# Rotation tables of a diagonal state-space layer, built by doubling on ScalarE and GpSimd in place of outer products on GpSimd alone

## What is computed

```python
mag = exp(lr * dt); abar = mag * (cos(li * dt) + 1j * sin(li * dt))
bu  = einsum('tgh,gph->tgp', u, bbar)        # drive of each state
x_t = abar * x_(t-1) + bu_t                  # scan over the 512 tokens
y   = Re(einsum('tgp,ghp->tgh', x, c)) + d * u
```

## Time and profile before

| | |
|---|---|
| runs, median (lowest to highest) | 3290.7 us (3290.01 to 3291.89) |
| the profiled execution | 3289.22 us, span 3287.4 us |
| PE, DVE, ACT, POOL busy in the profiled execution | 2939.9, 1758.0, 786.9, 531.4 us |
| the stage of interest | about 145 to 672 us of the span |

### The profile page before, as it was taken

How to read it: one execution, slowest core, us unless ns; L and a number is a source line. 1 busy time by engine, 2 the same in 40 slices (tenths; PEclk the granted TensorE clock), 3 DMA queues, 4 the chain that set the end, 5 groups by cost and what they waited for, 6 DMA issues and landing times. The chain is left out here.

```text
span 3287.4 us, 35120 instructions
## 1 busy us (share of the span) xinstructions
PE 2939.9 (89%) x13768; PEld 2205.4 (67%) x13768; DVE 1758.0 (53%) x2107; ACT 786.9 (24%) x1019; POOL 531.4 (16%) x411
## 2 busy tenths in 40 slices
PE   6999999987559958999999988899949999989897
PEld 4756666675228837888888765588828877765585
DVE  6799999965653365112553237522272157337433
ACT  4311111133432222111222213311122122213221
POOL 3365565515010041000000001000030000001000
PEclk8999999998679977999999999999959999999998
DMA  4667877761023141222433332222113254341321
GB/s 161 216 264 297 317 285 295 294 247 56 26 103 118 51 179 41 85 80 103 163 117 119 115 124 75 108 76 88 62 58 106 95 193 157 136 158 60 144 90 63
DMA packets 112852, 454.03 MB, mean 138 GB/s; under 512 B 11472, under 2 KB 20816, under 8 KB 76752
## 3 DMA queue, kind: packets, MB, share of 16 engines
q1 hardware_dynamic: 112720, 452.24, 37.5%
HBM read 380.36 MB, written 71.83 MB: 138 GB/s over the span
## 5 line engine op out<-in xcount | busy, mean ns | idle before, releaser
L2302 PE MATMUL ps<-h_hi,w_hi 128*128 128x512 f32 (+1 forms) x1792 | 661.6, 369 | 78.8 <-POOL h_lo L490 72.8
L2303 PE MATMUL ps<-h_lo,w_hi 128*128 128x512 f32 (+1 forms) x1792 | 645.0, 360 | 0.0
L2304 PE MATMUL ps<-h_hi,w_lo 128*128 128x512 f32 (+1 forms) x1792 | 640.8, 358 | 0.0
L2302 PEld LDWEIGHTS ps<-h_hi,w_hi 128*128 128x128 f32 x1792 | 344.9, 192 | 151.9 <-POOL h_lo L490 51.7
L384 PE MATMUL ps<-h_hi,w_hi 128*128 128x512 f32 (+1 forms) x1152 | 413.0, 358 | 37.7 <-DVE w_lo L337 37.7
L385 PE MATMUL ps<-h_lo,w_hi 128*128 128x512 f32 (+1 forms) x1152 | 412.2, 358 | 0.0
L2186 DVE TENSOR_TENSOR w_lo<-raw,w_hi 128x2048 fp32r<-128x2048 f32 x72 | 164.8, 2289 | 460.6 <-ACT w_hi L2137 460.6
L386 PE MATMUL ps<-h_hi,w_lo 128*128 128x512 f32 (+1 forms) x1152 | 410.0, 356 | 0.0
L2303 PEld LDWEIGHTS ps<-h_lo,w_hi 128*128 128x128 f32 x1792 | 346.1, 193 | 51.9 <-issue 6.0
L2304 PEld LDWEIGHTS ps<-h_hi,w_lo 128*128 128x128 f32 x1792 | 344.9, 192 | 51.3
L1475 POOL TENSOR_TENSOR wide<-ident_sb,stat 128x128 f32<-128x128 f32 x96 | 38.5, 401 | 1454.2 <-DVE stat L1535 1454.2
(11 more groups left out here) (305 smaller groups left out, 4333.7 us busy)
## 6 DMA issues: line engine op xcount, KB each, us to landing
raw<-w_in SPq DMA_DIRECT2D x112, 1024.0 KB, 5.1
raw<-ada_w SPq DMA_DIRECT2D x96, 1024.0 KB, 9.1
raw<-w_out SPq DMA_DIRECT2D x48, 1024.0 KB, 5.0
proj<-xw SPq DMA_DIRECT2D x60, 384.0 KB, 2.5
xw<-proj SPq DMA_DIRECT2D x70, 256.0 KB, 3.2
xw<-proj SPq DMA_DIRECT2D x46, 384.0 KB, 3.2
xw<-resid SPq DMA_DIRECT2D x8, 1536.0 KB, 12.2
proj<-wide SPq DMA_DIRECT2D x32, 256.0 KB, 11.2
```

The costliest lines, as they stand in the source:

```text
L2302: pe.matmul(a_[q], wh, h_hi[:, k, a:b], start=k == 0, stop=False)
L2303: pe.matmul(a_[q], wh, h_lo[:, k, a:b], start=False, stop=False)
L2304: ins = pe.matmul(a_[q], wl, h_hi[:, k, a:b], start=False, stop=k == KC - 1)
```

## The change

POOL no longer forms outer products. E[0..31] is copied to the head of `ee`, and four steps double the table: E[m..2m) = E[0..m) * E[m], for m = 32, 64, 128, 256. The factor E[m] is one number for each partition (the coarse power 1, 2, 4 or 8 of `e_sb`), so the four real products of a step are ACT activations with a scale from SBUF, into four half-size buffers `gt`; POOL does only the subtraction and the addition. ACT's `table(n+1)` stands between `w_hi` of slot n and the copies and `out_(n-1)` of that slot. Two semaphores are new: `turn_in` (ACT to POOL, products done) and `turn_out` (POOL to ACT, a step's sums done). Before the loop ACT does `table(0)` ahead of the first `w_hi`.

```diff
-            gt = [take(T) for _ in range(3)]
+            gt = [take(T // 2) for _ in range(4)]
...
-                        pool.wait_ge(st.sem, st.now)
-                        pool.tensor_tensor(g_[0], f_re, c_re, ALU.mult).then_inc(st.step(), 1)
...
-                        pool.tensor_tensor(ee[n % 2][1], gt[2], gt[1], ALU.add).then_inc(st.tell(e_ready, n + 1), 1)
+                        er, ei = ee[n % 2]
+
+                        pool.wait_ge(x_ready.h, x_ready.at(n - 1))
+                        pool.tensor_copy(er[:, 0:S_FINE], e_sb[:, j, 0, 0:S_FINE]).then_inc(st.step(), 1)
+                        pool.tensor_copy(ei[:, 0:S_FINE], e_sb[:, j, 1, 0:S_FINE]).then_inc(st.step(), 1)
+                        pool.wait_ge(st.sem, st.now)
+                        for s in range(4):
+                            m = S_FINE << s
+                            pool.wait_ge(turn_in.h, turn_in.at(4 * n + s + 1))
+                            pool.tensor_tensor(er[:, m:2 * m], gt[0][:, 0:m], gt[1][:, 0:m], ALU.subtract).then_inc(st.step(), 1)
+                            pool.wait_ge(st.sem, st.now)
+                            pool.tensor_tensor(ei[:, m:2 * m], gt[2][:, 0:m], gt[3][:, 0:m], ALU.add).then_inc(
+                                st.tell(e_ready, n + 1) if s == 3 else st.tell(turn_out, 3 * n + s + 1), 1)
+                            pool.wait_ge(st.sem, st.now)
...
+                    def table(n):
+
+                        i, j = divmod(n, 4)
+                        if j == 0:
+                            act.wait_ge(loaded[1].h, loaded[1].at(16 * (i + 1)))
+                        for s in range(4):
+                            m = S_FINE << s
+                            a = S_FINE + (1 << s)
+                            w_re, w_im = e_sb[:, j, 0, a:a + 1], e_sb[:, j, 1, a:a + 1]
+                            er, ei = (e_sb[:, j, c, 0:S_FINE] if s == 0 else ee[n % 2][c][:, 0:m] for c in range(2))
+                            if s:
+                                act.wait_ge(turn_out.h, turn_out.at(3 * n + s))
+                            else:
+                                act.wait_ge(e_ready.h, e_ready.at(n))
+                            act.activation(gt[0][:, 0:m], er, ACT.Copy, scale=w_re)
+                            act.activation(gt[1][:, 0:m], ei, ACT.Copy, scale=w_im)
+                            act.activation(gt[2][:, 0:m], er, ACT.Copy, scale=w_im)
+                            act.activation(gt[3][:, 0:m], ei, ACT.Copy, scale=w_re).then_inc(turn_in.h, 1)
+                    table(0)
                     for n in range(slots):
...
                         act.activation(w_hi[:, n % 2, :], raw[:, 0, :], ACT.Copy).then_inc(hi_done.h, 1)
+                        if n + 1 < slots:
+                            table(n + 1)
```

More of the change, by code:

```diff
@@ L206, in program @@
             "sq_added", "s_act", "s_vec", "ssm_in", "ssm_out", "cz_done", "e_done"))
+        turn_in, turn_out = count("turn_in"), count("turn_out")
         row_sums, sums_read, inverted = count("row_sums"), count("sums_read"), count("inverted")
@@ L965, in _ @@
                             pool.wait_ge(loaded[1].h, loaded[1].at(16 * (i + 1)))
[L966 to L970, removed]
@@ L971, in _ @@
-                        pool.wait_ge(st.sem, st.now)
-                        pool.tensor_tensor(g_[0], f_re, c_re, ALU.mult).then_inc(st.step(), 1)
-                        pool.tensor_tensor(g_[1], f_im, c_im, ALU.mult).then_inc(st.step(), 1)
-                        pool.wait_ge(st.sem, st.now)
-                        pool.tensor_tensor(g_[2], f_re, c_im, ALU.mult).then_inc(st.step(), 1)
-                        pool.wait_ge(x_ready.h, x_ready.at(n - 1))
-                        pool.tensor_tensor(ee[n % 2][0], gt[0], gt[1], ALU.subtract).then_inc(st.step(), 1)
@@ L979, in _ @@
-                        pool.wait_ge(st.sem, st.now)
-                        pool.tensor_tensor(g_[1], f_im, c_re, ALU.mult).then_inc(st.step(), 1)
-                        pool.wait_ge(st.sem, st.now)
-                        pool.tensor_tensor(ee[n % 2][1], gt[2], gt[1], ALU.add).then_inc(st.tell(e_ready, n + 1), 1)
+                        er, ei = ee[n % 2]
+                        pool.wait_ge(x_ready.h, x_ready.at(n - 1))
+                        pool.tensor_copy(er[:, 0:S_FINE], e_sb[:, j, 0, 0:S_FINE]).then_inc(st.step(), 1)
@@ L1140, in ssm_and_conditions @@
             for s, v in ((loaded[0], 32 * chunks), (loaded[1], 16 * chunks), (loaded[2], 16 * chunks), (b_ready, slots // 2),
-                         (b_read, slots), (e_ready, slots), (x_ready, slots), (y_out, chunks), (pair_used, slots // 2), (ada_used, per * slots), (ada_copied, 3 * LAYERS),
+                         (b_read, slots), (e_ready, slots), (turn_in, 4 * slots), (turn_out, 3 * slots), (x_ready, slots), (y_out, chunks), (pair_used, slots // 2), (ada_used, per * slots), (ada_copied, 3 * LAYERS),
                          (ada_turned, 3 * LAYERS), (mods_done, 3 * LAYERS), (hi_done, slots), (lo_done, slots),
```

## The result

Four runs of the changed kernel gave a median of 3390.9 us (3390.5 to 3395.4), four of the kernel before (the three above and one of 3284.6) 3290.4 us; the ratio is 1.031 (95% interval 1.029 to 1.033). Slower by 100.6 us, where 3391 us was forecast. The profiled execution took 3395.4 us, some 4 more than the median, so its stretches are a little long.

A forecast was written before the change was run, and what follows sets the result against it. DVE was taken as the bound, PE just behind. First chunk +18, six more +79, last +3 sum to +100, which on 3290.7 gives 3391 us; range 3325 to 3425.

The forecast's parts named there:

- the most that the change could bring: With DVE relieved, PE's 63.2 us a chunk against 65.2: 2.0 us for each of 8 chunks, about 16 us.
- walk of one chunk: Times through four slots from the end of the first drives: a chunk goes from 65.2 to 78.3 us, +13.1.
- POOL's last sums: End of each table, which `out_` was taken to follow; four later POOL operations meet DVE at 0.25 us each.
- The clock: PE's clock drops after long idleness at a boundary, costing its matmuls 1.0 + 0.5 = 1.5 us.
- the two ladders: Ordinary table: 11.4 us from the end of DVE's tile; first table of a chunk: 11.1 us from its powers landing.
- the low bound: Cheap end of every term, about +50 us, with powers landing 3 us earlier: worked out as 3320, given as 3325.
- two losses of its own: PE's main matmuls start late in each chunk: 5.0 us in slot 4i+1, 8.6 us at the boundary, slot 4i+3.
- the shut-out: A table's first POOL operations are kept from SBUF for all of DVE's `w_lo`, 2.3 us.
- Rival 2: Only boundaries cost, as `w_lo` does not shut POOL out: about +50, 3340 us; chance 0.25.
- Rival 1 (faster): `out_` is never late and PE becomes the bound: up to 16 us come back, 3275 us; chance 0.04.

The follow-up runs named there:

- experiment 1: The changed kernel with table(n+1) moved behind the copies and `out_(n-1)` on ACT; 3276.8 us, ratio 0.9962 to the kernel before.
- experiment 7: The changed kernel with six more unused ACT copies of 256 columns in each table; 3425.8 us, ratio 1.041 to the kernel before.
- experiment 8: The same six more ACT copies a table, in the changed kernel with table(n+1) moved behind `out_(n-1)`; 3279.9 us, ratio 0.9972.
- experiment 10: The changed kernel with three buffers for E and two tiles for the powers, `out_` still behind the table; 3285.1 us, ratio 0.9987.
- experiment 2: The kernel before without the outer products of 30 of its 32 tables, a one-column operation giving the signal; 3277.4 us, ratio 0.9966.
- experiment 4: The changed kernel with table(n+1) behind `out_(n-1)` and two tiles for the powers; 3277.5 us, ratio 0.9965.
- experiment 5: The changed kernel with table(n+1) behind `out_(n-1)` only in the last slot of each chunk (3, 7, ...); 3381.1 us, ratio 1.0281.
- experiment 6: The changed kernel with table(n+1) behind `out_(n-1)` only in the second slot of each chunk (1, 5, ...); 3371.2 us, ratio 1.0248.
- experiment 3: The changed kernel with two tiles for the powers, each load issued a chunk early; 3376.9 us, ratio 1.0271.
- experiment 9: The changed kernel with three buffers for E, so table(n+1) waits for DVE's tile n-2, `out_` still behind it; 3344.0 us, ratio 1.017.

## Why the prediction was right, and where not

The forecast and its mechanism held. PE waits for `out_`, `out_` stands behind the ladder on ACT (experiments 1, 7 and 8), and the ladder begins late for two reasons: table(n+1) waits for DVE's tile n-1, and at a boundary for the powers. Taking both away with the order left as it is (experiment 10) brings back 106 us where 101 had been lost, so all of it and a little of the gain. What the forecast called the most that the change could bring, about 16 us, measured about 12 (experiments 1, 2, 4). It was read from one chunk: from drives to drives the mean of six is 64.9 us in the kernel before, not 65.2, and 63.7 in experiment 1, where PE waits for nothing after slot 0, not 63.2.

Its walk of one chunk, against the chunk that begins at 313.64 in the trace after, the end of slot 8's drives:

| | forecast | trace |
|---|---|---|
| DVE's tile of slot 4i ends | 10.8 | 11.8 |
| main matmuls of 4i+1, late by | 23.6, 5.0 | 23.7, 5.1 |
| next drives done | 36.6 | 38.4 |
| powers land | 52.0 | 52.5 |
| main matmuls of 4i+3, late by | 63.8, 8.6 | 63.3, 6.3 |
| chunk (to the end of the next chunk's drives) | 78.3 | 78.6 |

The agreement is better than the working deserves: three of its terms were off and cancel, which is luck.
- **The end of the ladder that counts.** The working let `out_` wait for POOL's last sums. ACT never waits for those: it is free after its last products, 1.5 us earlier. To that point the ladder took 10.8 us from DVE's tile, where the same terms less the last sums would give about 9.4; POOL's operations between DVE's wait longer than the 0.25 each that was taken (L978 of 128 columns 1.25 us above, against 0.45 for the shortest of its size in this stage and 0.40 in the earlier trace rows). The same meetings explain POOL's 197 us: at the shortest time of each shape its ten operations a table would make 125.
- **A wait that was not seen.** DVE's last products wait for PE's state outputs of the pair before (L1087, 15 times, 20.7 us, all in even slots). They come within PE's main matmuls of the even slot, and DVE, no longer late, is there first. With 1.7 of such a wait in slot 8 the tile ends at 11.8 instead of 10.8 us.
- **The clock.** It was charged at 1.5 us, at boundaries and in the first chunk only. The stretches after a wait of 5.07 us in slot 9, and after the 5.54 us of slot 11, two us each:

```profile
337.40:339.40 2.00, 2.00 (x5) 1.61 (x6) 1.74 (x2) 0.00 (x0) 1.24 (x3) 0.50 0.99 254
339.40:341.40 2.00, 2.00 (x7) 1.58 (x7) 0.00 (x0) 0.00 (x0) 0.22 (x2) 0.67 0.99 397
...
376.96:378.96 2.00, 2.00 (x7) 1.61 (x6) 1.06 (x5) 2.00 (x5) 1.12 (x4) 0.50 0.93 380
378.96:380.96 2.00, 2.00 (x7) 1.52 (x6) 1.78 (x1) 0.31 (x2) 1.47 (x2) 0.50 0.05 9
380.96:382.96 2.00, 2.00 (x9) 1.65 (x8) 0.00 (x0) 1.06 (x4) 0.68 (x3) 0.82 0.60 94
```

Half speed (1.2 GHz) and two thirds in the mean cost 1.0 + 0.7 = 1.7 us in the one, 1.0 + 1.0 + 0.4 = 2.4 us in the other. The main matmuls of slot 9 from their first to the next drives, after and before:

```profile
337.35:350.03 12.68, 12.68 (x48) 10.09 (x48) 4.08 (x3) 4.90 (x13) 3.96 (x8) 0.87 1.00 388
...
304.14:315.29 11.15, 11.15 (x49) 8.94 (x49) 11.01 (x13) 1.92 (x1) 6.04 (x5) 1.00 0.93 360
```

The stage as a whole is longer by 105 us in the profiled executions (first main matmul of slot 31 at 766.3 against 661.3), and the two traces divide it without a rest. PE's waits account for 74 (72.9 + 11.3 + 3.9 against 13.7). The main matmuls of slots 0 to 30, measured like the two above, took 407.6 us against 377.6: 30 more. In the 16 slots behind a wait of 3.9 us or more they took 1.5 to 2.8 us longer than without one (slot 1 had lost 1.4 before as well); the even slots from 2 on kept their 13.2. The forecast's 100 were 88 of waits (the gain taken off) and 12 of clock. So the waits were charged 14 too high and the clock 18 too low.

Of smaller slips, the terms of the two ladders add to 11.5 and 11.2, not 11.4 and 11.1, and the low bound is worked out as 3320 but given as 3325; neither decides anything.

**What the walk hid.** It gave each chunk two losses of its own, 5.0 and 8.6, and the expectations of experiments 5 and 6 took them for separate. They are places where one lateness shows. With the ladder in front, drives, DVE's tile (11.8), ladder (10.8), `out_` with `y_copy` (1.1), odd main matmuls at their dropped clock (12.7) and the next drives (2.0) form a loop over two slots: 38.4 us from the drives of slot 8 to those of slot 10, against 31.6 of PE's own work. In experiment 3, where no load stands in the way, the chunk is 76.3 us, close to the loop twice. Every stall of PE in an odd slot is slack for the even one behind it. Take away one stall, and the next table ahead of an `out_` is late (slot 8 above). Only a cut through the loop in every slot frees PE: by order (experiment 1), or by a third buffer that takes DVE's tile out of it (experiment 9, with the boundary's load cut by 10).

The lock rule of the Trainium skill ("SBUF — State Buffer", Who interferes with whom) holds in the rows: `w_lo` takes 2.29 us, and POOL's copy beside it is shut out for its whole length. That the shut-out costs a ladder about 2.3 us was right, but not that every ordinary ladder has it. It falls on table(4i+2) in all eight chunks, for which PE waits in slot 4i+1, and on two others of the 32. Table(4i+3), which the walk charged with it too, starts before its `w_lo` from the second chunk on; PE does not wait there, so the sum did not suffer. Rival 2, which wanted no shut-out, would have needed more than that: by the walk's own numbers a table ready at 20 still leaves the main matmuls 2.7 us late. The Trainium skill ("ScalarE: Activation LUTs", What ACT_TABLE_LOAD costs) gives 93 ns for a per-partition operand on top of 186 + 0.833 ns a column. The groups of the changed kernel agree, 307 and 493 ns at 32 and 256 columns (an estimate from the page's figures makes it 306 and 492):

```profile
L1016 ACT ACTIVATE xw<-xw 128x256 f32<-128x256 f32 x32 | 15.8, 493 | 0.0
...
L1016 ACT ACTIVATE xw<-xw 128x32 f32<-128x32 f32 x32 | 9.8, 307 | 0.0
```

Rival 1 (faster) named the right price and lacked its condition; experiment 1 shows that the condition was a place in a queue and not the length of the ladder.

## What to carry to other kernels

Before work is moved to an engine that is idle most of the time, ask what stands behind the new work in that engine's queue and who waits for it: ACT was idle for five sixths of the stage, and the change still cost 100 us, because a copy of 0.6 us came to stand behind a chain that waits for two other engines and a load. Put what another engine waits for ahead of a chain that itself waits. When a stall has been found, look for the loop it is part of before pricing its removal, since a fix in one place of a loop may only move the wait.

## What the runs showed of the hardware

The kernel before showed half speed after 6.3 us of idleness of PE; these runs show it after much less. In slot 6 of experiment 7 PE was idle for 2.07 us (to 285.74), and the stretch from 288 to 290 was granted 0.50; a wait of 1.28 us in the kernel before (slot 12) was followed by 1.00. After 4.08 us in slot 8 of the version with the move in the last slot it was 0.50 for at least 4 us; in slot 9 of the change it was back at 0.67 in the mean within 4 us, after 5.07 us idle. The loss does not grow with the wait: behind 7.53 us (slot 15 of the change) the main matmuls took 1.7 us longer, behind 4.89 (slot 17) 2.8. What decides how long it lasts, these runs do not show. Experiment 7, then the version with the last slot:

```profile
288.00:290.00 2.00, 2.00 (x7) 1.54 (x6) 0.00 (x0) 0.00 (x0) 0.20 (x1) 0.50 1.04 397
...
311.00:313.00 2.00, 1.96 (x5) 1.61 (x6) 0.00 (x0) 2.00 (x3) 1.14 (x2) 0.50 0.99 414
313.00:315.00 2.00, 2.00 (x6) 1.53 (x5) 0.00 (x0) 0.54 (x3) 0.00 (x0) 0.50 1.00 422
```
